# A mixture-of-experts layer on one core: six instead of five row gathers issued ahead of the scatters on GpSimd's queue

## The reference, cut to what matters

```python
scores = jax.nn.sigmoid(h @ w_router)                      # 512 tokens x 64 experts
_, top_idx = lax.top_k(scores + router_bias, TOP_K)        # 8 experts for each token
top_w = top_s / jnp.sum(top_s, axis=-1, keepdims=True) * ROUTE_SCALE
# for expert e, of width 256:
hmid = jax.nn.silu(xb @ w_gate_e) * (xb @ w_up_e) * gate_e
out += hmid @ w_down_e
# plus a shared expert for all tokens, and the residual
```

## Time and profile before

| | |
|---|---|
| median of three runs | 1127.37 us (1125.38 to 1129.15) |
| the profiled execution, its own time | 1129.43 us |
| its span in the trace | 1127.4 us |
| PE busy | 97% |
| DVE busy | 78% of the span, about 95% in the expert stage |
| ACT busy | 65% of the span |
| POOL busy | 28% |
| granted clock of TensorE, mean | 0.987 |

### The profile page before, as it was taken

How to read it: one execution, slowest core, us unless ns; L and a number is a source line. 1 busy time by engine, 2 the same in 40 slices (tenths; PEclk the granted TensorE clock), 3 DMA queues, 4 the chain that set the end, 5 groups by cost and what they waited for, 6 DMA issues and landing times.

```text
span 1127.4 us, 18998 instructions
## 1 busy us (share of the span) xinstructions
PE 1091.3 (97%) x5774; PEld 895.9 (79%) x5774; DVE 882.1 (78%) x1405; ACT 737.1 (65%) x1304; POOL 320.2 (28%) x293
## 2 busy tenths in 40 slices
PE   7999999999999999999999999999999999999995
PEld 5888978777777877577887888888888888888884
DVE  6544376478865835579999999999999999999993
ACT  5334364544346512149887888888888888888883
POOL 0221012000000001125345344454346536333342
PEclk7999999999999999999999999999999999999998
DMA  5433312421522183549999999999999999999962
GB/s 181 139 76 112 112 38 76 150 75 38 135 110 94 39 344 141 227 174 403 382 392 361 377 378 377 381 368 386 375 381 377 357 387 377 379 384 391 381 207 36
DMA packets 69704, 284.69 MB, mean 253 GB/s; under 512 B 16611, under 2 KB 19179, under 8 KB 44700
## 3 DMA queue, kind: packets, MB, share of 16 engines
q1 hardware_dynamic: 51228, 250.50, 57.0%
q0 software_dynamic: 18432, 33.61, 12.6%
HBM read 279.79 MB, written 37.81 MB: 282 GB/s over the span
## 4 chain that ended last, share of the span: by engine, by line
PE 46%; DMA 35%; DVE 7%; issue 4%; POOL 3%; ACT 2%; POOLq 0%; SPq 0%; ACTq 0%; DVEq 0%
DMA out<-arena,idxs 33%; PE bank L1601 20%; PE bank L1770 9%; PE bank L1784 5%; PE bank L1744 3%; PE bank L1550 3%; POOL turn L589 2%; PE bank L1758 2%; DVE w_lo L1066 1%; PE bank L1798 1%; ACT arena L765 1%; DMA arena<-in_w_out 1%; DVE gu_parts L1392 1%; DMA arena<-hn_dram,idxg 1%; DMA arena<-in_x 1%
## 5 line engine op out<-in xcount | busy, mean ns | idle before, releaser
L1770 PE MATMUL bank<-gu_parts,xT_parts 128*128 128x512 f32 x1280 | 339.0, 395 | 2.1 <-DVE xT_parts L1385 1.0
L1770 PEld LDWEIGHTS bank<-gu_parts,xT_parts 128*128 128x128 f32 x1280 | 235.3, 188 | 49.1 <-DVE xT_parts L1385 1.2
L589 POOL TENSOR_TENSOR turn<-minus_half 16x1 f32<-16x1 f32 x128 | 103.4, 807 | 350.3 <-DMA out<-arena,idxs 286.2
L1784 PE MATMUL bank<-w_lo 128*128 128x512 f32 x804 | 201.6, 399 | 1.0 <-DVE w_lo L1398 1.0
L1784 PEld LDWEIGHTS bank<-w_lo 128*128 128x128 f32 x804 | 146.3, 188 | 29.7 <-DVE w_lo L1398 1.2
L1601 PE MATMUL bank<-w_hi,hT_hi 128*128 128x512 f32 (+1 forms) x320 | 125.9, 393 | 3.3 <-DVE arena L1341 1.9
L1601 PE MATMUL bank<-w_lo,hT_hi 128*128 128x512 f32 (+1 forms) x320 | 123.2, 385 | 0.0
L1601 PE MATMUL bank<-w_hi,hT_lo 128*128 128x512 f32 (+1 forms) x320 | 123.2, 385 | 0.0
L599 POOL DMA_INDIRECT out<-arena,idxs x64 | 114.5, 1789 | 25.9 <-issue 23.3
L1392 DVE TENSOR_TENSOR gu_parts<-arena_x,gu_parts 128x1024 fp32r<-128x1024 f32 x96 | 116.8, 1217 | 0.9 <-ACT gu_parts L931 0.9
L1392 DVE TENSOR_TENSOR gu_parts<-arena,gu_parts 128x1024 fp32r<-128x1024 f32 x96 | 116.8, 1217 | 0.6 <-ACT gu_parts L931 0.6
(11 more groups left out here) (226 smaller groups left out, 1941.8 us busy)
## 6 DMA issues: line engine op xcount, KB each, us to landing
arena<-in_w_gate_e SPq DMA_DIRECT2D x32, 1024.0 KB, 8.9
arena<-in_w_up_e SPq DMA_DIRECT2D x32, 1024.0 KB, 12.1
arena<-in_w_down_e SPq DMA_DIRECT2D x32, 1024.0 KB, 7.2
arena_x<-in_w_gate_e SPq DMA_DIRECT2D x32, 1024.0 KB, 9.1
arena_x<-in_w_up_e SPq DMA_DIRECT2D x32, 1024.0 KB, 12.0
arena_x<-in_w_down_e SPq DMA_DIRECT2D x32, 1024.0 KB, 7.1
arena<-in_w_in SPq DMA_DIRECT2D x14, 1024.0 KB, 5.4
arena<-in_w_gate SPq DMA_DIRECT2D x8, 1024.0 KB, 5.7
```

Source lines behind the costliest of these rows:

```text
L589: nc.gpsimd.tensor_tensor(turn[:], minus_half[0:16, 0:1], minus_half[0:16, 0:1], ALU.add).then_inc(turns, 1)
L1770: last = nc.tensor.matmul(out_, a[:, PER * c + j, :], b[c][:, :, j, :], start=(c == 0 and j == 0 and i == 0), stop=(c == CHUNKS - 1 and j ...
L1784: last = nc.tensor.matmul(psY[h][0:rows, :], midT[n][a][:, j, 0:rows], w[b][:, j, h * 512:(h + 1) * 512], start=(j == 0 and k == 0), stop= ...
```

## The change

GpSimd's list is changed. The gather of expert k+6 instead of k+5 is issued behind the scatter of expert k, and six gathers instead of five are issued in front of the first scatter. The slot of the buffer and the numbers of the `turns` semaphore are changed to fit. Nothing changes on the other engines.

```diff
-            for k in range(5):
+            AHEAD = 6
+            for k in range(AHEAD):
                 gather_k(k, k % 4, k)
             for b in based:
                 pool.wait_ge(b, 8 * SH)
 
             def pair(k, u):
-                scatter_k(k, u, 5 + 2 * k)
-                gather_k(k + 5, (u + 1) % 4, 6 + 2 * k)
+                scatter_k(k, u, AHEAD + 2 * k)
+                gather_k(k + AHEAD, (u + AHEAD) % 4, AHEAD + 1 + 2 * k)
 
             for k in range(4):
                 pair(k, k)
-            with pool.Fori(1, (E - 5) // 4) as m:
+            with pool.Fori(1, (E - AHEAD) // 4) as m:
                 for u in range(4):
                     pair(4 * m + u, u)
-            for k in range((E - 5) // 4 * 4, E - 5):
+            for k in range((E - AHEAD) // 4 * 4, E - AHEAD):
                 pair(k, k % 4)
             more = pool.value_load(rounds_i[0:1, 0:1], min_val=0, max_val=ROUNDS - 1)
-            for k in range(E - 5, E):
-                scatter_k(k, k % 4, 5 + 2 * (E - 5) + k - (E - 5))
+            for k in range(E - AHEAD, E):
+                scatter_k(k, k % 4, E + k)
```

## The result

The changed kernel took 1134.62 us (median of 8 runs, 1133.39 to 1140.32), the kernel before 1126.21 us (median of 8, 1124.82 to 1129.15). The ratio is 1.0078, with a 95% interval of 1.0063 to 1.0094. The prediction gave "faster" 0.45 and "slower" 0.12, and its range ended at 1130.5 us. The profiled execution of the changed kernel took 1135.44 us, with a span of 1133.4 us and a mean granted clock of 0.988.

A forecast was written before the change was run, and what follows sets the result against it. PE's pace was taken as the bound, the scatters running close: a 4.6 us gain, 0 for the new wait and 0.2 lost at the start gave -4.4 us, taken as 4.0 from 1127.37: 1123.4 us, range 1118.5 to 1130.5.

The forecast's parts named there:

- First step: Expert stage: gathers issued one step earlier end PE's five waits for them, a gain of 5.0 to 5.9 us.
- Second step: Expert stage: PE then arrives sooner at split rows and ACT's results, and new waits there take back up to 0.8 us.
- the scatters are the real bound: Rival, chance 0.30: the scatters' own pace bounds the expert stage, about 1 us of gain stays, 1126.5 us.
- Third step: POOL in the loop: the gather waits 0.1 to 2 us more for its index, hidden before the next scatter, 0 us.
- that rival: Chance 0.12: gather turns fall into DVE's subtractions, up to 1.1 us per stalled step; 12 such steps give 1136 us.
- Fourth step: Start of the expert stage: scatter 0 goes out later behind gather 5, at about 520.1, costing 0.2 us.

The follow-up runs named there:

- e17: Changed kernel, GpSimd's loop written out, row numbers found one expert earlier, the first early index in the middle of expert 0: 1129.47 us, 1.0000.
- e18: Kernel before (five ahead), GpSimd's loop written out, row numbers found one expert earlier, the first early index in the middle of expert 0: 1129.00 us, 0.9996.
- e11: Kernel before (five ahead) with GpSimd's loop written out and no turns ahead of the experts' gathers and scatters: 1127.53 us, 1.0002.
- e5: The changed kernel measured again with no edit, beside the kernel before: 1133.10 us, 1.0045.
- e12: Changed kernel (six ahead) with GpSimd's loop written out and no turns ahead of the experts' gathers and scatters: 1130.42 us, 1.0023.
- e10: Kernel before (five ahead) with two more turns ahead of each scatter: 1136.06 us, 1.0091.
- e2: Changed kernel with GpSimd's loop written out and each expert turn a memset that reads no SBUF, in place of the addition: 1129.62 us, 1.0020.
- e1: Changed kernel with GpSimd's loop written out: 1131.47 us, 1.0032.
- e4: Kernel before (five ahead), each gather from the sixth on also waiting for the next expert's index: 1130.94 us, 1.0031.
- e9: Changed kernel with DVE writing the index of expert k+3 in the middle of expert k, 6 us later: 1159.51 us, 1.0277.
- e14: Kernel before (five ahead), GpSimd's loop written out, row numbers found one expert earlier from the start on: 1133.27 us, 1.0052.
- e13: Changed kernel (six ahead), GpSimd's loop written out, row numbers found one expert earlier from the start on: 1134.09 us, 1.0071.
- e16: Kernel before (five ahead) with GpSimd's loop written out and nothing else: 1126.59 us, 1.0004.

## Why the prediction was wrong

**First step (the five waits for gathers, 5.0 to 5.9 us).** The waits did go, in the changed kernel and in e17. The time did not come. e17 against e18 measures what the sixth gather is worth when nothing else is in its way: 1.0000 against 0.9996, nothing, with some 3 us of doubt either way by the two intervals. This is the second error, hidden under the first.

**Second step (what is late next, 0.8 us).** The mechanism was right and the size wrong: with the gathers in time, PE waits for DVE behind ACT behind a scatter, and that takes back 2.4 of 2.8 us in the pair of profiles, not 0.8 of 5.5. I priced it by ACT's old waits over all steps, 0.15 us each, while PE's steps without a gather wait lost 4.1 us and its idle rows showed 1.0. The short waits cost nothing and those from 1.4 us on cost about 0.9 us each (13.7 us for 16 in the changed kernel). And a gather is late in a step whose turn was held, and there the scatter behind it is late too. The trace of before shows both in one step: four of the five steps that waited for a gather have a wait of ACT for a scatter of 1.5 to 2.1 us in them (the copies at 598.1, 764.1, 851.9 and 881.7), and the step behind loses only 0.1 us, as PE had been held up already. Removing the gather's wait leaves the scatter's, which had only been second to it. The rival "the scatters are the real bound" (0.30) is right for these steps. For the others it is not: e11 shortens their chain and wins nothing.

**Third step (the new wait is hidden, 0 us).** This is the step that failed. The wait itself, 0.8 us in 14 steps, lies in POOL's idle time as I said. What I costed at nothing was what starts behind it. Since the index releases the turn, the turn starts inside DVE's one-hot, 0.2 us ahead of the run, with POOL idle, and in 13 of 14 cases it loses the whole run. I knew the mechanism and gave it 0.12, because turns that were 0.1 us or more ahead of the run had all passed. I measured the margin to the run and left out the one-hot in front of it. And what those turns had in common in the rows was that POOL was still at the scatter's descriptors when they came. The changed kernel has 13 held turns more in its profile; if the sixth gather is worth nothing, as e17 against e18 has it, the whole 8.4 us are theirs, 0.65 us each (in e5 5.9 us for 14, 0.42 each; in e12 0.2 each). My price of up to 1.1 us was the delay of the scatter; e10 and ACT's waits show that a delay there reaches PE only in part. I expected 12 such steps in that rival, and the trace has 13 more than before; its 1136 us came close by luck, through two errors that cancel, a price too high and a gain of 4 us that wasn't there.

**Fourth step (the start, 0.2 us).** No loss shows: 31.3 us from the transposes of expert 0 to those of expert 3 in both kernels. It came by another way than I said. No turn ahead of scatter 0 was held; it went out at 517.7 instead of 520.1 and took 10.7 us to land, and ACT's copy of result 2 did not wait for it.

The rule of the Trainium skill that I weighed (SBUF — State Buffer, section "Who interferes with whom") named the right conflict. For the turns that pass, the trace agrees: the turn at 603.91 starts inside the one-hot and ends 0.04 us behind it. The row of the held turn again goes beyond it: 6.02 us, the rest of the one-hot and five subtractions, not one instruction. The same section says, marked as inferred, that such subtractions leave descriptor writing alone, since that needs the write interface. The trace of e2 doesn't agree: descriptors took 6.29 us while DVE did nothing but such a run.

What stays open: what decides, where the one-hot ends, whether the turn gets in. With the run 0.20 to 0.26 us behind the turn, none of 89 turns that came while POOL was at a scatter's descriptors was held, in the changed kernel, e5, e1 and e4 together. Of those that came with POOL idle 14 of 15 were held in the changed kernel and 14 of 16 in e5, but 8 of 20 in e1 and 8 of 21 in e4, whose rows look the same. It also stays open why scatters need 11.0 us with four result buffers.

## What to carry to other kernels

Before costing a new wait at nothing, ask what else the releasing engine does right behind the release: an operation released by VectorE starts beside VectorE's next instructions, and on GpSimd that can cost a whole run of them. In a queue served in order, a prefetch in front of a serial chain is not free slack: if it is late, the chain behind it is late (0.6 us a step on average in e9). Don't price waits by their mean: in the changed kernel ACT's waits of up to 1.2 us cost next to nothing and those of 1.4 us and more nearly all that was lost. And a wait that ends last may cover another in the same step; price its removal from a step in which both are late.

## What the runs showed of the hardware

A small GpSimd addition with inputs in SBUF, or the descriptors of an indirect DMA (e2), can be held for as long as VectorE runs back-to-back operations with two SBUF inputs: 5.5 to 6.8 us beside a run of five subtractions, with or without the one-hot in front, until one with an input in PSUM comes. Of the turns that waited for the index 13 of 14 were held in the changed kernel, 13 of 15 in e5, but 7 of 18 in e4; of those that came straight behind a scatter's descriptors 6 of 59 in the kernel before, five of them with the run at most 0.04 us behind them and one inside it.

TensorE's granted clock fell from full speed (2.4 GHz) to half (1.2 GHz) behind an idle time of 4.52 us in e14 (0.50 from 492 to 495 us), and in e13 behind two of 0.87 and 0.52 us within 2 us (0.50 from 657 to 659 us), after which six matmuls took 2.19 us instead of 1.63 and the step 13.28 us instead of 9.53:

```profile
655.00:660.00 5.00, 4.49 (x13) 3.49 (x14) 5.00 (x9) 3.13 (x5) 2.31 (x3) 0.66 1.01 378
```

In the kernel before and in the changed one, waits of up to 1.8 us did not bring the clock down in the expert stage. In e9 one of 1.68 us (at 1068.6) didn't either, and one of 1.75 us (at 821.9) did. Where it fell, the step lost more than the wait: 15.77 - 10.72 = 5.05 us for 4.52 us in e14 (10.72 us is the same step in e16), 13.28 - 9.53 = 3.8 us for 1.39 us in e13.
